# Even and odd mixers with two step slots a projection tile, another order of columns and heads, score buffers by item, and keys scaled by logarithm and exponential

## The chip, the cores and the metric

The kernel runs on one core of a Trainium2 chip. The metric is the device time of one execution in microseconds. The engines are TensorE (PE, with its weight loads PEld), VectorE (DVE), ScalarE (ACT), GpSimd (POOL) and SyncE (SP), which issues the DMA transfers here. Each engine runs its own instructions strictly in the order of the program; waits between engines are on semaphores.

## What is computed

Two blocks of a transformer run one after the other on 256 tokens of 1024 channels, all in float32. The first block has a convolution layer and a dilated attention layer, each followed by a gated feed-forward (gu0/dn0, gu1/dn1). The second block, which the change touches, is

```python
h = rms_norm(x, g) * (1 + scale) + shift        # scale, shift from "ada", a product of the condition
x = x + gate * (mixer(h) @ w_out)               # layer 0: even mixer, layer 1: odd mixer
x = x + gate2 * swiglu(...)                     # gu2/dn2 and gu3/dn3

def even_mixer(h):   # 23 tiles of 128 columns
    # 4 differential heads: two queries, two keys of 64, RMS-normed; a = softmax(1) - lam * softmax(2)
    # 8 sparse heads: one shared key and value; keys are picked by an index score (8 heads of
    #   relu(iq . ik) * iw, top 64 of each row)
def odd_mixer(h):    # 12 tiles; 16 heads, 4 shared keys and values, window of 128, one sink each
```

In both mixers every query and key vector of 64 is divided by its root mean square before the scores.

## The kernel before

Every product is `product(name, ...)`. The weights stand in one long list of 128x128 blocks; 8 blocks make a unit. SyncE loads a unit into `raw`, ScalarE rounds it into `whi` (`highs`, line 793), VectorE forms the remainder `wlo` (`lows`, line 1144). TensorE forms each block of a product from three matmuls (line 486): high by high, low by high, high by low. A tile is 128 output columns; with 8 blocks in its contraction it takes 24 matmuls. The first `lead` tiles of a product (2 in the mixers and their output products) are computed block row by block row together, since the parts of their input arrive one after another; the later ones follow one by one. The mixers use three PSUM banks for tiles, two for scores, one for norms and transposed values, one for transposes, one for weighing.

The mixers, `even()` and `odd()` in each engine's program, hang attention steps onto the tiles. `AFTER_E` and `AFTER_O` are tables written by hand: for each tile number, the steps that every engine issues behind that tile. Numbers from 23 (even) and 12 (odd) on stand for the block rows of the lead tiles of the output product, `oute` or `outo`. The steps of a differential head are dscore, dexp, dfact, dturn, dweigh, dnorm, dout; of a pair of sparse heads sscore, sexp, sfact, two sturn, sweigh; index, top and pick make the selection; of a pair of odd heads score, exp, fact, two turn, weigh. Scores, transposes and weighing are TensorE's, the exponentials and the copies out of PSUM are ScalarE's, maxima, factors and remainders are VectorE's; sfact and the odd fact are multiplied by GpSimd (`factors`, line 1678).

`project(...)` handles a tile m itself. VectorE takes it out of PSUM, times the norm of its token (`taken`, line 1491), as the last thing behind tile m. ScalarE squares it in slot m+1 (`TQ`). TensorE sums the squares by a product with `bones` (line 652) behind tile m+2, or transposes a value tile (line 649). ScalarE then takes, for a query, `Ln` and `Exp` with scale -0.5, and for a key `Sqrt`; VectorE in slot m+3 multiplies the query by the result, or for a key forms the reciprocal (line 1482) and multiplies. ScalarE copies the key with its gain in slot m+4. `log_exp()` (line 853) loads the table for `Ln` and `Exp` behind slot 14 of the even mixer and slot 5 of the odd.

`total(i)` sums the squares for the token norms of the whole layer behind tile 0; ScalarE takes the root and VectorE the reciprocal (`inverse`, line 1196) before tile 0 can be taken. `shift(i)` writes two columns for the shift beside the input of a product, which the first matmul waits for. `residual` adds an output tile to X, scales it for the next product and splits it, with one weight unit's `lows` a tile. Scores lie in two buffers `eS` (even) and three `oS` (odd), transposed weights in five `eP` and six `oP`.

## Time and profile before

| | |
|---|---|
| median of 3 runs | 1331.71 us (1327.31 to 1332.41) |
| profiled execution: time, span | 1326.97 us, 1325.7 us |
| mean granted TensorE clock | 0.963 of full |
| busy: PE, DVE, ACT, POOL | 1215.2, 970.9, 657.6, 110.3 us |
| even mixer, first matmul to the first of gu2 | about 631 to 804 us |
| odd mixer, first matmul to the first of gu3 | about 1011 to 1133 us |
| DMA | 259.36 MB, mean 196 GB/s |

The span is from the first to the last instruction of the profiled execution. A clock of 1.0 is the full one, 2.4 GHz; the other level is 0.5. Busy shares over the whole span mix stages with different limits, so the rows further below are taken by stage.

### The profile page before, as it was taken

The numbers are of one execution on the slowest core, as the hardware profiler recorded it, in microseconds if no ns is written. First come the engines' busy times: TensorE is split into PE (matmuls) and PEld (weight loads), VectorE is DVE, ScalarE is ACT, GpSimd is POOL, SyncE is SP. The second block draws the span as 40 slices with busy tenths as digits, with TensorE's granted clock in tenths as the row PEclk, the third lists the DMA queues.
The fourth block names the chain that finished last, engine by engine and source line by source line (L and its number), as shares of the span: only waits on it lengthen the run. The fifth ranks groups of instructions, "written<-read, shape, count | busy, mean of one in ns | idle before, by whom it ended". The sixth has DMA issues, their size and how long they took to land.

```text
span 1325.7 us, 24775 instructions
## 1 busy us (share of the span) xinstructions
PE 1215.2 (92%) x9796; PEld 1152.7 (87%) x9796; DVE 970.9 (73%) x1860; ACT 657.6 (50%) x1139; POOL 110.3 (8%) x106
## 2 busy tenths in 40 slices
PE   4978899999998999999878788999989868999999
PEld 4957899999987999999868578999989747999999
DVE  5966598779777888879799557888876734666743
ACT  5326554444446544454566554544444845554531
POOL 2001100002001100004000121000011113100000
PEclk9999899999999999999999789999999967999999
DMA  7587687778853778778634125887855512555552
GB/s 260 158 202 101 227 303 254 258 249 277 268 172 119 229 252 265 241 254 272 201 112 139 64 68 189 260 264 241 307 181 179 161 43 66 175 186 180 188 192 65
DMA packets 81126, 259.36 MB, mean 196 GB/s; under 512 B 8904, under 2 KB 20424, under 8 KB 81012
## 3 DMA queue, kind: packets, MB, share of 16 engines
q1 hardware_dynamic: 81012, 257.79, 61.5%
q8 instruction: 78, 1.28, 0.4%
q14 instruction: 36, 0.29, 0.1%
HBM read 252.68 MB, written 5.08 MB: 194 GB/s over the span
## 4 chain that ended last, share of the span: by engine, by line
PE 70%; DVE 18%; issue 4%; ACT 3%; POOL 1%; DMA 1%; DVEq 0%; ACTq 0%
PE ps L486 62%; DVE wlo L1144 5%; DVE aacc L1150 2%; PE ps L580 1%; DVE CV L1150 1%; POOL oS L1678 1%; PE ps L584 1%; PE ps L545 1%; ACT HH L793 1%; DVE X L1150 1%; DMA raw<-wall 1%; PE ps L576 1%; PE ps L575 1%; DVE HL L1144 1%; DVE tn L1147 1%
## 5 line engine op out<-in xcount | busy, mean ns | idle before, releaser
L486 PE MATMUL ps<-HH,whi 128*128 128x256 f32 (+1 forms) x2152 | 622.8, 289 | 41.0 <-DVE HL L1144 18.4
L486 PE MATMUL ps<-HH,wlo 128*128 128x256 f32 (+1 forms) x2152 | 614.3, 285 | 0.0
L486 PE MATMUL ps<-HL,whi 128*128 128x256 f32 (+1 forms) x2152 | 613.7, 285 | 0.0
L793 ACT ACTIVATE whi<-raw 128x1024 fp32r<-128x1024 f32 x363 | 381.1, 1057 | 344.4 <-PE ps L486 339.1
L1144 DVE TENSOR_TENSOR wlo<-raw,whi 128x1024 fp32r<-128x1024 f32 x363 | 443.9, 1227 | 42.9 <-ACT whi L793 42.4
L486 PEld LDWEIGHTS ps<-HH,whi 128*128 128x128 f32 x2152 | 414.9, 193 | 56.9 <-ACT HH L793 24.5
L486 PEld LDWEIGHTS ps<-HL,whi 128*128 128x128 f32 x2152 | 414.7, 193 | 0.3
L486 PEld LDWEIGHTS ps<-HH,wlo 128*128 128x128 f32 x2152 | 414.3, 192 | 0.0
L486 PE MATMUL ps<-GH,whi 128*128 128x256 f32 x704 | 198.2, 282 | 0.6 <-DVE bcol L1370 0.5
L486 PE MATMUL ps<-GL,whi 128*128 128x256 f32 x704 | 197.4, 280 | 0.0
L486 PE MATMUL ps<-GH,wlo 128*128 128x256 f32 x704 | 197.4, 280 | 0.0
L486 PEld LDWEIGHTS ps<-GH,whi 128*128 128x128 f32 x704 | 132.8, 189 | 2.9 <-issue 1.7
L1150 DVE SCALAR_TENSOR_TENSOR aacc<-araw,cond,aacc 128x512 f32<-128x512 f32 x168 | 132.4, 788 | 3.4
L486 PEld LDWEIGHTS ps<-GL,whi 128*128 128x128 f32 x704 | 132.9, 189 | 0.0
L486 PEld LDWEIGHTS ps<-GH,wlo 128*128 128x128 f32 x704 | 132.7, 189 | 0.0
L1678 POOL TENSOR_TENSOR HL<-tn,HH 128x256 fp32r<-128x256 f32 x24 | 24.5, 1019 | 749.5 <-ACT HH L793 749.5
L1369 DVE TENSOR_TENSOR tmp<-ps,RST 128x256 f32<-128x256 f32 x88 | 37.1, 423 | 49.0 <-PE ps L486 48.4
L793 ACT ACTIVATE HH<-tn 128x256 fp32r<-128x256 f32 x68 | 28.4, 417 | 88.9 <-DVE tn L1147 84.1
L1144 DVE TENSOR_TENSOR tmp<-ps,RST 128x256 f32<-128x256 f32 x104 | 43.3, 419 | 33.8 <-PE ps L486 33.4
L1678 POOL TENSOR_TENSOR SQA<-SQA,ts 128x256 f32<-128x256 f32 x48 | 55.1, 1147 | 48.5 <-ACT ts L793 47.5
L793 ACT ACTIVATE GH<-tmp 128x256 fp32r<-128x256 f32 x88 | 35.4, 402 | 22.6 <-DVE tmp L1144 17.9
L1144 DVE TENSOR_TENSOR HL<-ps,HH 64x256 fp32r<-64x256 f32 (+1 forms) x24 | 9.5, 421 | 46.5 <-ACT HH L793 46.5
(208 smaller groups left out, 1038.2 us busy)
## 6 DMA issues: line engine op xcount, KB each, us to landing
raw<-wall SPq DMA_DIRECT2D x363, 512.0 KB, 4.3
araw<-ada SPq DMA_DIRECT2D x96, 512.0 KB, 4.7
UR<-uscr SPq DMA_DIRECT2D x24, 142.0 KB, 3.2
scratch<-bvec SPq DMA_DIRECT2D x1, 3072.0 KB
oBB<-kbias SPq DMA_DIRECT2D x16, 192.0 KB, 2.6
aTB<-scratch SPq DMA_DIRECT2D x12, 128.0 KB, 2.5
X<-x_in SPq DMA_DIRECT2D x2, 512.0 KB, 6.5
out<-X SPq DMA_DIRECT2D x8, 128.0 KB, 3.1
```

The lines of the kernel that those rows point to most:

```text
L486: ins = pe.e.matmul(o, l, r, start=(kt == p.order[0] and i == 0), stop=(kt == p.order[-1] and i == 2))
L545: ins = pe.e.matmul(bk[32 * r:32 * r + 32, 0:T], DG[j][:, 8 * r + m, :], UR[n % 3][:, r, 4 * m:4 * m + T], start=(m == 0), stop=(m == 7))
L575: pe.e.matmul(bk[:, 0:128], q[:, 0:128], k[:, 0:128], start=True, stop=True)
L576: return pe.e.matmul(bk[:, 128:384], q[:, 128:256], k[:, 0:256], start=True, stop=True)
L580: ins = pe.e.transpose(bk[:, i * P:(i + 1) * P], s[:, i * P:(i + 1) * P], ident[:, :])
L584: pe.e.matmul(o, v(0), pt[:, 0:256], start=True, stop=False)
L793: ac.then_inc(ac.e.activation(o, i, func, **kw), sem)
L1144: dv.then_inc(dv.e.tensor_tensor(o, a, b, op), sem)
L1147: dv.then_inc(dv.e.tensor_scalar(o, a, s, s2, op) if op2 is None else dv.e.tensor_scalar(o, a, s, s2, op, op2), sem)
L1150: dv.then_inc(dv.e.scalar_tensor_tensor(out=o, in0=a, scalar=s, in1=b, op0=op, op1=op2), sem)
L1369: dv.e.tensor_tensor(t[:, :], ps[:, 0:T], rooted(name)[:, :], ALU.mult)
L1678: po.then_inc(po.e.tensor_tensor(o, a, b, op), sem)
```

## The change

1. Slots: the mixers now count two slots a tile. Slot 2m lies in the middle of tile m (behind its fourth block), slot 2m+1 behind it. Slots from 46 (even) and 24 (odd) on are the block rows of the output product. The tables are built by `differ`, `sparse` and `attend` from a start slot for each head. Slot 2 is issued between the two lead tiles' end and slot 3.
2. `project`: TensorE's norm product or transpose of tile m moves to slot 2m+2, in the middle of tile m+1; ScalarE's square to slot 2m+1, `Ln`/`Exp` to 2m+2, the key copy to 2m+4; VectorE's product to slot 2m+3. `taken` stands before `project` and the steps in slot 2m+1.
3. Orders: the columns of both mixers are in another order (keys, queries and values nearer to the heads that need them), and differential and sparse heads alternate.
4. Keys use `Ln` and `Exp` as queries do; the `Sqrt` and VectorE's `reciprocal` go. `log_exp()` moves to slot 1, and the constants with lambda's exponential to slot 3.
5. Buffers: three `eS` and `eST` by item (numbered in order of scores), eight `oP`; `eIQ` and `eRL` share their memory with later buffers.
6. `oute` and `outo` have three lead tiles. `shift(i)` is issued at the start of the residual before it, and waits for less of the ada product.

```diff
-EVEN = (17, 18, 19, 20, 21, 22, 4, 5, 6, 7, 16, 0, 8, 1, 9, 2, 10, 3, 11, 12, 13, 14, 15)
-ODD = (8, 9, 10, 11, 0, 1, 2, 3, 4, 5, 6, 7)
+EVEN = (17, 18, 19, 20, 21, 22, 4, 0, 8, 5, 1, 16, 12, 9, 13, 6, 2, 14, 7, 3, 15, 10, 11)
+ODD = (8, 0, 1, 10, 2, 3, 9, 4, 5, 6, 7, 11)
...
-    Product("mixe", 23, KD, 2, banks=(0, 1, 2)), Product("oute", 8, KD, 2, banks=(0, 1, 2)),
+    Product("mixe", 23, KD, 2, banks=(0, 1, 2)), Product("oute", 8, KD, 3, banks=(0, 1, 2)),
...
-    Product("mixo", 12, KD, 2, banks=(0, 1, 2)), Product("outo", 8, KD, 2, banks=(0, 1, 2)),
+    Product("mixo", 12, KD, 2, banks=(0, 1, 2)), Product("outo", 8, KD, 3, banks=(0, 1, 2)),
...
+def differ(k, at, weigh):
+    return (chain(weigh, ("dout", k, 2), ("dnorm", k, 1), ("dweigh", k, 0))
+            + chain(at, ("dturn", k, 3), ("dfact", k, 2), ("dexp", k, 1), ("dscore", k, 0)))
+
+
+def sparse(k, at, turn=4, weigh=6):
+    return chain(at, ("sweigh", k, weigh), ("sturn", 2 * k, turn), ("sturn", 2 * k + 1, turn + 1), ("sfact", k, 2),
+                 ("sexp", k, 1), ("sscore", k, 0))
+
+
+def attend(k, at, turns=(4, 5), weigh=6):
+    return chain(at, ("weigh", k, weigh), ("turn", 2 * k, turns[0]), ("turn", 2 * k + 1, turns[1]), ("fact", k, 2),
+                 ("exp", k, 1), ("score", k, 0))
+
+
+AFTER_E = by_slot(
+    [(3, "const", 0), (13, "gain", 0)] + [(13 + k, "index", k) for k in range(4)] + [(17 + k, "top", k) for k in range(8)]
+    + [(25, "pick", 0)] + differ(0, 18, 22) + differ(1, 24, 29) + sparse(0, 28) + sparse(1, 32) + differ(2, 36, 45)
+    + sparse(2, 38, 4, 6) + differ(3, 42, 48) + sparse(3, 44))
+AFTER_O = by_slot(
+    [(3, "const", 0)] + attend(0, 6) + attend(1, 8) + attend(2, 12) + attend(3, 14) + attend(4, 18, (4, 5), 7)
+    + attend(5, 20, (3, 4), 5) + attend(6, 22, (3, 3), 4) + attend(7, 24, (3, 3), 4))
...
+            eS = [sb(f"eS{i}", [P, 2, 384], F32, st) for i in range(3)]
...
+            oP = [sb(f"oP{i}", [P, 384], F32, st) for i in range(8)]
...
+                    if kt == p.order[3] and middle and (nt == 0 or nt >= p.lead):
+                        middle(nt)
...
-                m = s - 2
-                if not 0 <= m < len(tiles.kind) or tiles.kind[m] == "plain":
+                m = (s - 2) // 2
+                if s % 2 or not 0 <= m < len(tiles.kind) or tiles.kind[m] == "plain":
...
+            def slotted(slot):
+
+                def after(nt):
+                    if nt == 1:
+                        slot(2)
+                    slot(2 * nt + 1)
+                return dict(middle=lambda nt: slot(2 * nt), after=after)
...
-            def project(tiles, s, gain, outs):
+            def project(tiles, name, s, gain, outs):
 
                 k = tiles.kind
-                m = s - 4
-                if 0 <= m < len(k) and k[m] == "key":
-                    ac.wait_ge(S.kr, 2 * tiles.no[m] + 2)
-                    pieces = outs(m)
-                    for n, (rs, o) in enumerate(pieces):
+                m = (s - 4) // 2
+                if s % 2 == 0 and 0 <= m < len(k) and k[m] == "key":
+                    ac.wait_ge(S.kr, tiles.no[m] + 1)
+                    for rs, o in outs(m):
                         ins = ac.e.activation(o, TM[m % 6][rs, :], ACT.Copy, scale=gain(m)[rs, :])
                     ac.then_inc(ins, S.kc)
-                m = s - 2
-                if 0 <= m < len(k) and k[m] != "plain":
+                m = (s - 2) // 2
+                if s % 2 == 0 and 0 <= m < len(k) and k[m] != "plain":
                     ac.wait_ge(S.bon, tiles.bank[m] + 1)
-                    q = TQ[tiles.norm[m] % 3]
                     if k[m] == "value":
                         act(outs(m), bank[5][:, 0:T].rearrange("p (a b) -> p a b", a=2), ACT.Copy, S.b5)
-                    elif k[m] == "key":
-                        act(q[:, :], bank[5][:, 0:T], ACT.Sqrt, S.b5, bias=epsb[:, 0:1], scale=1.0 / 64)
                     else:
+                        q = TQ[tiles.norm[m] % 3]
                         act(q[:, :], bank[5][:, 0:T], ACT.Ln, S.b5, bias=epsb[:, 0:1], scale=1.0 / 64)
                         ac.settle()
                         act(q[:, :], q[:, :], ACT.Exp, S.qex, scale=-0.5)
-                m = s - 1
-                if 0 <= m < len(k):
+                m = s // 2
+                if s % 2 and 0 <= m < len(k):
                     t, b = TM[m % 6], bcol[m % 6]
-                    ac.wait_ge(S.ev, slot_of("mixe" if tiles is TE else "mixo", m) + 1)
+                    ac.wait_ge(S.ev, slot_of(name, m) + 1)
                     if k[m] == "plain":
...
-                    project(TE, s, gain_of, outs)
-                    if s == TE.col[16] + 4:
                         log_exp()
+                    project(TE, "mixe", s, gain_of, outs)
...
+                if i is not None and i >= 4:
+                    shift(i)
...
-            def project(tiles, name, s, out_of):
-
-                m, k = s - 3, tiles.kind
-                if 0 <= m < len(k) and k[m] in ("query", "key"):
+            def project(tiles, s, out_of):
+
+                m, k = (s - 3) // 2, tiles.kind
+                if s % 2 and 0 <= m < len(k) and k[m] in ("query", "key"):
                     t, b, q = TM[m % 6], bcol[m % 6], TQ[tiles.norm[m] % 3]
+                    dv.wait_ge(S.qex, tiles.norm[m] + 1)
                     if k[m] == "query":
-                        dv.wait_ge(S.qex, tiles.no[m] + 1)
                         stt(out_of(m), t[:, :], b[:, 0:1], q[:, :], ALU.add, ALU.mult, S.qf)
                     else:
-                        dv.wait_ge(S.b5, tiles.bank[m] + 1)
-                        dv.then_inc(dv.e.reciprocal(q[:, :], q[:, :]), S.kr)
-                        dv.settle()
                         stt(t[:, :], t[:, :], b[:, 0:1], q[:, :], ALU.add, ALU.mult, S.kr)
...
                 def slot(s):
-                    if s < 23:
-                        lows(low_to("mixe", s))
-                    if s == 0:
+                    if s % 2 and s < 46:
+                        lows(low_to("mixe", s // 2))
+                    if s == 1:
                         dv.wait_ge(S.twa, 1)
                         dv.wait_ge(S.tot2, 1)
                         tt(TMP[8][:, :], TMP[8][:, :], bank[6][:, 0:T], ALU.add, S.twb)
                         inverse(5)
                         inverse(6)
-                    elif s <= 4:
-                        for kt in (2 * s - 2, 2 * s - 1):
+                    if s % 2 and s < 46:
+                        taken(TE, "mixe", s // 2)
+                    if s in (5, 7, 9, 11):
+                        for kt in (s - 5, s - 4):
                             dv.wait_ge(S.rst, 7)
                             dv.wait_ge(S.sq2, kt + 1)
                             stt(X[:, kt, :], X[:, kt, :], V("fin", kt), RST[0][:, :], ALU.mult, ALU.mult, S.xf)
-                    project(TE, "mixe", s, lambda m: eQK[:, EVEN[m] if EVEN[m] < 8 else EVEN[m] - 4, :])
+                    project(TE, s, lambda m: eQK[:, EVEN[m] if EVEN[m] < 8 else EVEN[m] - 4, :])
                     for w, k in AFTER_E.get(s, ()):
                         step(w, k)
-                    if s < 23:
-                        taken(TE, "mixe", s)
-
-                for s in range(23):
+
+                for s in range(46):
                     slot(s)
-                residual("oute", 5, lambda nt: mod(0, 2, nt), ALU.mult, lambda kt: slot(23 + kt))
+                residual("oute", 5, lambda nt: mod(0, 2, nt), ALU.mult, lambda kt: slot(46 + kt))
 
             def odd():
                 def step(what, hp):
                     s2, ST = oS[hp % 3], oST[hp % 3]
```

## Rows read from the trace of the kernel before

**Rows 1.** Even mixer: stretch, us; PE, PEld, DVE, ACT, POOL busy; clock, DMA, GB/s

```profile
668.00:696.40 28.40, 20.33 (x155) 17.75 (x154) 27.70 (x55) 18.46 (x32) 0.00 (x0) 0.92 0.35 112
696.40:735.00 38.60, 34.34 (x247) 30.81 (x248) 36.55 (x128) 24.48 (x64) 0.00 (x0) 0.93 0.44 135
735.00:781.60 46.60, 33.02 (x166) 23.63 (x164) 18.65 (x47) 24.05 (x72) 7.45 (x8) 0.71 0.13 44
781.60:803.60 22.00, 17.96 (x150) 17.76 (x150) 18.62 (x30) 12.62 (x25) 10.81 (x9) 1.00 0.49 150
```

**Rows 2.** The same for the odd mixer

```profile
1038.00:1060.00 22.00, 18.50 (x143) 15.43 (x142) 16.17 (x64) 16.70 (x49) 4.98 (x4) 1.00 0.54 168
1060.00:1111.40 51.40, 35.83 (x179) 24.14 (x179) 15.65 (x71) 22.60 (x73) 12.16 (x13) 0.67 0.12 39
1111.40:1132.50 21.10, 19.05 (x156) 18.71 (x156) 16.92 (x29) 13.59 (x26) 10.84 (x9) 1.00 0.44 131
```

**Rows 3.** Chain of waits (start, us, what), and TensorE's timeline

```profile
630.69 0.49 issue
...
703.57 2.87 PE ps L486 x24
...
706.66 0.43 PE ps L575 x4
707.09 0.43 PE ps L576 x4
...
711.12 1.14 DVE wlo L1144
...
1021.01 0.45 PE L652 MATMUL ps<-tmp,bones 128*128 128x256 f32 x1 [0.36 <-ACT tmp L793]
```

**Rows 4.** ScalarE's timeline: start us, us, instruction

```profile
638.12 1.28 ACT L793 ACT_TABLE_LOAD   x1
...
1043.26 0.49 ACT L793 ACTIVATE tmp<-tmp,bcol 128x256 f32<-128x256 f32 x1
1043.65 0.39 ACT L793 ACTIVATE oS<-oS,oST 128x128 f32<-128x128 f32 x1
...
1045.51 1.05 ACT L793 ACTIVATE whi<-raw 128x1024 fp32r<-128x1024 f32 x1
```

**Rows 5.** VectorE's timeline in both mixers

```profile
668.00 1.75 DVE L1482 RECIPROCAL tmp<-tmp 128x256 f32<-128x256 f32 x1
...
693.45 0.62 DVE L1519 MAX8 eM<-eSW 128x8 f32<-128x128 f32 x2
...
694.77 0.41 DVE L1491 TENSOR_TENSOR tmp<-ps,RST 128x256 f32<-128x256 f32 x1
...
707.73 0.17 DVE L1554 RECIPROCAL eST<-eST 128x4 f32<-128x4 f32 x1
...
709.33 0.28 DVE L1390 CUSTOM_DVE_ANT_0 eS<-ps,eBB 128x128 f32<-128x128 f32 x1
...
740.71 1.01 DVE L1150 SCALAR_TENSOR_TENSOR eS<-eDS,ps 128x384 f32<-128x384 f32 x2
...
742.88 0.42 DVE L1491 TENSOR_TENSOR tmp<-ps,RST 128x256 f32<-128x256 f32 x1
...
1066.52 0.41 DVE L1491 TENSOR_TENSOR tmp<-ps,RST 128x256 f32<-128x256 f32 x1
```

**Rows 6.** GpSimd's and VectorE's timeline while both work

```profile
1050.55 2.60 POOL L1678 TENSOR_TENSOR oS<-oS,oST 128x256 f32<-128x256 f32 x2 [46.25 <-DVE oST L1637]
...
1050.78 1.47 DVE L1144 TENSOR_TENSOR wlo<-raw,whi 128x1024 fp32r<-128x1024 f32 x1
1052.17 1.26 DVE L1150 SCALAR_TENSOR_TENSOR oQ<-tmp,bcol 128x256 f32<-128x256 f32 x1
```

**Rows 7.** VectorE's first residual instruction in each mixer's tail

```profile
782.24 0.48 DVE L1150 SCALAR_TENSOR_TENSOR X<-ps,MOD,X 128x256 f32<-128x256 f32 x1 [0.71 <-PE ps L486]
...
1113.01 0.48 DVE L1150 SCALAR_TENSOR_TENSOR X<-ps,MOD,X 128x256 f32<-128x256 f32 x1 [0.72 <-PE ps L486]
```

More of the change, by code:

```diff
@@ L199, with chain @@
[L199 to L207 removed]
+def chain(at, *steps):
+    return [(at + later, what, k) for what, k, later in steps]
@@ new lines, in by_slot @@
+def by_slot(steps):
+    slots = {}
+    for s, what, k in sorted(steps, key=lambda x: x[0]):
+        slots.setdefault(s, []).append((what, k))
+    return slots
+def differ(k, at, weigh):
[4 more added lines that the diff above has]
+                 ("sexp", k, 1), ("sscore", k, 0))
@@ L258, with counted, item @@
 STEPS_O = [x for s in sorted(AFTER_O) for x in AFTER_O[s]]
-SCORES_E = [(w, k, g) for w, k in STEPS_E if w in ("index", "dscore", "sscore") for g in range(2)]
-BANK6_E = [x for x in STEPS_E if x[0] in ("dturn", "dnorm", "sturn")]
-BANK7_E = [(w, k) for w, k in STEPS_E if w in ("dweigh", "sweigh")]
+def counted(**by):
+    n, at = 0, {}
+    for what, k in STEPS_E:
+        if what in by:
+            n += by[what]
+            at[what, k] = n
+    return at
+SCORES_E = [(w, k, g) for w, k in STEPS_E if w in ("index", "dscore", "sscore") for g in range(2)]
+ITEMS_E = counted(dscore=1, sscore=1)
+EM_E = counted(dscore=5, sscore=5)
+EX_E = counted(dexp=4, sexp=4)
+FACT_E = counted(dfact=6, sfact=1)
+TURNED_E = counted(dturn=1, sturn=1)
+BANK6_E = counted(dturn=1, dnorm=1, sturn=1)
+WEIGHED_E = counted(dweigh=1, sweigh=1)
+YHH_E = counted(dout=1, sweigh=1)
+BANK7_E = counted(dout=1, sweigh=1)
+def item(what, k):
+    return ITEMS_E[what[0] + "score", k // 2 if what == "sturn" else k] - 1
 class Queue:
@@ L707, in step @@
+                    if what == "sweigh":
+                        for g in range(2):
+                            pe.wait_ge(S.b6, BANK6_E["sturn", 2 * k + g])
+                            ins = weigh(bank[7][rows64(g), 0:T], lambda tt: eV[:, tt, 512:576],
+                                        eP[(TURNED_E["sturn", 2 * k + g] - 1) % 5])
+                        pe.then_inc(ins, S.ewe)
                     if what == "dnorm":
-                        pe.wait_ge(*free6(AT_BANK6[what, k]))
+                        pe.wait_ge(S.b6, BANK6_E[what, k] - 1)
@@ L718, in after, with slot @@
-                def after(s):
-                    if s == 0:
+                def slot(s):
+                    if s == 1:
                         total(4)
@@ L772, in after @@
                         step(w, k)
-                product("mixo", HH[NORM_SET[6]], HL[NORM_SET[6]], T + 2, norm_ready(6), after)
-                product("outo", HH[YO_SET], HL[YO_SET], T, lambda kt: pe.wait_ge(S.ohl, kt + 1), None, lambda kt: after(12 + kt))
+                product("mixo", HH[NORM_SET[6]], HL[NORM_SET[6]], T + 2, norm_ready(6), **slotted(slot))
+                product("outo", HH[YO_SET], HL[YO_SET], T, lambda kt: pe.wait_ge(S.ohl, kt + 1), None, lambda kt: slot(24 + kt))
             convolution()
@@ L1114, in slot @@
                 def slot(s):
-                    if s < 12:
-                        highs(split_to("mixo", s))
-                    if s == 0:
+                    if s % 2 and s < 24:
+                        highs(split_to("mixo", s // 2))
+                    if s == 1:
                         norm_root(6)
-                    project(TO, s, gain_of, outs)
-                    if s == TO.col[9] + 4:
                         log_exp()
+                    project(TO, "mixo", s, gain_of, outs)
                     for w, k in AFTER_O.get(s, ()):
                         step(w, k)
-                for s in range(12):
+                for s in range(24):
                     slot(s)
-                residual("outo", 7, lambda kt: slot(12 + kt))
+                residual("outo", 7, lambda kt: slot(24 + kt))
             convolution()
@@ L1617, in step @@
                     M, NM, DEN, FA, SE = (ST[:, i, :] for i in range(5))
+                    if what == "const":
+                        gains(1, 1)
+                        tt(gqk[:, 2:3], V("qnc"), V("knc"), ALU.mult, S.gqk)
+                        dv.wait_ge(S.mm, end_mm("dn2"))
+                        for i in range(2):
+                            dv.then_inc(dv.e.tensor_copy(oSK[:, :, i:i + 1], row[:, 256:272].unsqueeze(2)), S.sk)
                     if what == "score":
```

239 lines of the change are left out of this document (100 added, 139 removed).

## The prediction

> **What bounds it now.** I read the table of stretches first. The even mixer [rows 1] and the odd one [rows 2] are where TensorE is less than full; the feed-forward stages between them are solid matmul. In the even mixer three regimes follow each other. From 668 to 735 us VectorE is busy 64 of 67 us: it sets the pace. From 735 to 781.6 us no engine is full (TensorE 33 of 46.6, VectorE 18.7), the granted clock averages 0.71, and what ends last is a chain of attention steps. From 781.6 to 803.6 VectorE works through the residual. The odd mixer shows the same: 51.4 us at a clock of 0.67, with the projections mostly done and the heads following one behind the other.
>
> Then the chain of waits and the engines' timelines, for prices [rows 3 to 5]. TensorE: a tile is 8 blocks, 24 matmuls, 2.87 us; a pair of score products 0.86. VectorE, counted from start to start so that overlap isn't paid twice: a weight rest (wlo) 1.13, taking a tile 0.41, one round of the top-k 1.32, the differential factors 1.6, the sparse scores 2.17, a key's reciprocal 1.75. ScalarE: the exponentials of one head pair 1.86.
>
> **The change, part by part.**
>
> *Keys by logarithm and exponential.* The reciprocal of 1.75 us leaves VectorE for 5 keys in the even and 2 in the odd mixer: 12.2 us of VectorE work, against one more ScalarE instruction of about 0.4 us per key. The even ones fall in the stretch where VectorE sets the pace, so this is a real gain, about 8.7 us, inside the sum below. In the odd mixer VectorE is not full [rows 2], and it is worth little.
>
> *Tables and shifts.* The load of 1.28 us at 638.12 [rows 4] goes, since lambda's exponential moves behind the square roots. ScalarE would still wait for VectorE's sum there, so I count 0.35 us to 0.8 us. The shift columns are now written ahead of the residual: the 0.49 us of issue at 630.69 [rows 3] is two tiny VectorE instructions in front of the first matmul, and the same stands in front of gu2, mixo and gu3. Four times 0.49. The start of the even mixer thus comes 0.85 us earlier by the time tile 3 starts (the two gains overlap in part).
>
> *Two slots a tile.* This is the heart, and it has a price. Before, the norm matmul of tile m stood after tile m+2, so TensorE had two tiles of work while VectorE took the tile and ScalarE squared it. Now it stands in the middle of tile m+1: 1.44 us after the end of tile m. VectorE takes tile m behind the steps of slots 2m-1 and 2m and a weight rest; if those include factors that wait for an exponential, a loop closes: square of tile m-1 (0.45), exponentials (1.86), factors (0.2 sparse or 1.6 differential), scores if any (1.33 or 2.17), weight rest and taking (1.54), back to the square of tile m. That is 4.2 to 9 us with hops of 0.05, against 3.3 to 6 us of TensorE work in the same tile.
>
> I followed the even order through. VectorE takes tile 6 at about 658.5 (one step of the ada product lies ahead of it). Tiles 7 to 12, where top-k rounds and differential head 0 fill VectorE: 5.6, 5.9, 6.8, 5.8, 6.1, 7.0 us, sum 37.2. Six tiles with the loop (13, 15, 17, 19, 20, 22): 5.5, 4.7, 6.6, 9.5, 4.7, 9.0, sum 40.0. Four where VectorE waits for scores placed in a tile's middle (14, 16, 18, 21): 5.4, 7.8, 5.3, 6.9, sum 25.4; two of these hold an ada step of 1.45. One of them spelled out, tile 19: square 0.45, copy of a transpose 0.4, exponentials 1.86, logarithm and exponential of a query norm 0.83, copy of a weighed head 0.3 on ScalarE, then on VectorE its rest 0.34, factors 1.6, sparse scores 2.17, weight rest and taking 1.54: 9.5. (ScalarE's single instructions on 256 columns count 0.3 to 0.45, by the one of 0.49 in [rows 4], overlap taken off.) All together 102.6, so tile 22 is taken at 761.1 instead of 742.88 [rows 5]: 18.2 us later.
>
> But only one differential head and two half-done sparse ones are then left. From 761.1: ScalarE's identity, square, copy, exponentials and two norm instructions, then head 2's product, split and rest, 5.2 us, to 766.3; head 3's weighing, square, norm and split behind it, 4.1, to 770.4; block row 3 (1.1), the last sparse head (1.3) and block rows 4 to 7 (4.3), to 777.1. The last factors on GpSimd (2.6 us [rows 6]) run beside it. 16.0 us to the end of the lead of 24 blocks. Before it was 39.4 us, from 742.88 to the first residual at 782.24 [rows 7]. So the lead ends 5.2 us earlier.
>
> *Three lead tiles.* The residual is paced by VectorE: 21.4 us from 782.24 to the end of the last stretch of [rows 1], for 8 tiles, 6 weight rests and an ada step. With three lead tiles one rest (1.13) is done before the lead ends, and the shift's 0.3 to 0.5 is gone: -1.4 us. All three banks are then full, so TensorE waits about 0.5 us for the first residual; VectorE's list is longer anyway (20 us against 14.2 for five tiles), which hides it. Even mixer: -6.6 us.
>
> *Odd mixer.* Here is a new wait. The first tile is a key, and its norm matmul stands in slot 2, straight behind the two lead tiles. Before, tile 2 was computed while the root, the reciprocal and the square of tile 0 ran, and even then the matmul came 0.36 us after TensorE was free, at 1021.01 [rows 3]. Now TensorE waits some 3.0 us with tile 2 still ahead of it. The even mixer starts with plain tiles and is spared. Then the loop again, head by head: the tiles are taken at about 1031.9 (tile 3), 1038.2, 1042.8, 1050.1, 1058.2, 1062.7, 1072.2, 1080.3 and 1086.3, against 1066.52 for the last before [rows 5]: 19.8 us later. From there, half of the heads being done, 22.1 us to the end of the lead at 1108.4, against 46.5 us (1066.52 to 1113.01, [rows 5, 7]): 4.6 us earlier. The residual gives 1.6 as above. Odd mixer: -6.2 us.
>
> *At no cost:* the score buffers by item (three instead of two) remove waits that in my walk are never last; oP with 8 buffers likewise; moving the bias loads on the sync queue keeps them ahead of weight loads that are several tiles early (DMA share 0.35 to 0.44, [rows 1]). If a bias load were late, its head would wait for the landing once.
>
> *GpSimd beside VectorE.* Factors now run beside weight rests and residual products. A product of 0.48 us took 1.26 beside them [rows 6]: +0.78 us at most, 12 times, 0 to 9 us; I take 0.3 each where it lies in a loop, within the walk. The Trainium skill ("SBUF — State Buffer", SBUF: two separate sides) says the port pair shared by VectorE and GpSimd is an exclusive lock, the loser waiting out the whole instruction. The row agrees for the second product, which ends just behind GpSimd; by the rule alone every such meeting could cost up to a full GpSimd instruction.
>
> *Clock.* At 0.5 of the full clock a tile costs twice 2.87. The stretch from 668 to 735, with TensorE about three quarters occupied, kept 0.92 to 0.93 [rows 1]; the new tiles are as dense (about 77 us of TensorE work in 102). I add 1.5 us.
>
> **Sum.** 1326.97 (the profiled execution's own time) - 6.6 - 6.2 + 1.5 = 1315.7. That execution is at the low end of the runs shown (median 1331.71), which by itself asks for up to 4 us more; I say 1316.
>
> **Rivals.**
>
> *The loops hide.* If ScalarE and VectorE run ahead more than my walk lets them, each tile costs only the larger of its TensorE and VectorE lists: about 85 instead of 102.6 us in the even mixer, some 12 us less in the odd one. Then 1316 - 29 = 1287, or half of it, 1300. For it: both lists sum to about 122 us by the prices above, for a mixer of 173 us (630.69 to 803.60, [rows 1, 3]). Against it: every queue is strictly in order, and each factor step stands ahead of a taking.
>
> *No change.* The tiles lengthen by 18 to 20 us in each mixer and the tails shorten by 23 to 24; these are differences of large terms. Two more microseconds on each of six loop tiles, or the full 9 us beside GpSimd, and nothing is left: 1325 to 1335. The port rule ends here too (0.03 of the 0.15 below): if each of the 12 pairs of GpSimd products, 2.6 us by [rows 6], held VectorE up for 1.5 us, that is 18 us, and 1334. This is the mechanism that the page just named describes.
>
> *Slower: the clock.* The gaps of 2 to 3 us in every tile pull the granted clock down, as between 1060 and 1111 us [rows 2]. If the new stretches (102 and 59 us, with 77 and 45 us of TensorE work) ran at 0.75, the work would take 26 and 15 us more; about 40% of it would fall into gaps, so +24: 1340. It decides from a mean clock of about 0.87 there.
>
> **Chances.** Forecast, 1305 to 1325: 0.45. Loops hidden, below 1305: 0.30. No change: 0.15. Slower: 0.10. Half a per cent, 6.7 us, is about what a measurement of this kernel tells from nothing: faster 0.75, same 0.15, slower 0.10. The range 1291 to 1333 leaves about 0.1 on each side.
>
> **What would show it.** Right: no reciprocal on keys; one idle gap of about 3 us on TensorE near 1017, ended by the first square; gaps of 1 to 3 us in the middle of most mixer tiles, released by ScalarE's square; tile 22 taken near 761; a tail of about 16 us in place of 39; residuals 20 and 18 us. Wrong: no gaps in the tiles (1300 or less); a clock under 0.87 from 690 to 770; a load of tables inside the mixers; or a tail still above 25 us.

## The result, and the profile after

The changed kernel takes 1319.81 us (median of 5 runs, 1318.96 to 1324.01), the kernel before 1331.71 (its five runs lie between 1327.31 and 1332.41); the ratio is 0.9929, interval 0.9911 to 0.9947, which is 9.5 us. The profiled execution took 1320.58 us, with a span of 1319.2 and a mean granted clock of 0.972. The forecast was 1316 in a range of 1291 to 1333, so time, sign and range held. Of the steps behind it the walk through the tiles held, and the price of the joints and the length of the tails did not.

First the table of stretches (columns as in [rows 1]), three of the even mixer and one of the odd. A joint below is the place where one product ends and the next begins.

```profile
668.00:700.00 32.00, 21.74 (x149) 19.03 (x147) 29.57 (x106) 16.78 (x42) 0.00 (x0) 0.95 0.36 111
700.00:735.00 35.00, 30.34 (x209) 25.54 (x209) 19.93 (x49) 20.50 (x55) 5.22 (x4) 0.90 0.34 103
735.00:782.00 47.00, 34.65 (x229) 29.79 (x230) 24.58 (x62) 24.91 (x64) 5.22 (x4) 0.89 0.28 84
...
1082.00:1109.30 27.30, 21.29 (x128) 16.87 (x129) 7.77 (x26) 12.93 (x35) 4.11 (x4) 0.75 0.22 67
```

VectorE was busy 64 of 67 us from 668 to 735 us in the kernel before [rows 1]. Now it is busy 29.6 of the first 32 us and 19.9 of the 35 behind them: no engine is full from 700 us on. But the even mixer's lead (the first tiles of its output product, which run together) does not end earlier. VectorE's timeline, last tile taken and first residual in each mixer (compare [rows 5, 7]):

```profile
762.65 0.42 DVE L1532 TENSOR_TENSOR tmp<-ps,RST 128x256 f32<-128x256 f32 x1
...
782.12 0.48 DVE L1194 SCALAR_TENSOR_TENSOR X<-ps,MOD,X 128x256 f32<-128x256 f32 x1 [1.76 <-PE ps L521]
...
1081.34 0.42 DVE L1532 TENSOR_TENSOR tmp<-ps,RST 128x256 f32<-128x256 f32 x1
...
1109.26 0.48 DVE L1194 SCALAR_TENSOR_TENSOR X<-ps,MOD,X 128x256 f32<-128x256 f32 x1 [2.18 <-PE ps L521]
```

Tile 22 is taken 20 us later than before, and the tail shrank from 39.4 to 19.5 us: the first residual moved by 0.1 us. What TensorE waited for from 640 to 782 us, the two largest entries (us in total, times, longest):

```profile
PE ps L689 <- ACT tmp L840: 14.3, 10, 2.8
PE ps L686 <- ACT tmp L840: 7.3, 4, 3.7
```

L689 is the norm matmul in the middle of the next tile, L686 the transposition of a value tile in the same place; both wait for ScalarE's square or identity, and ScalarE's own wait for VectorE's taking is 43.1 us in 16 gaps in the same stretch. In the odd mixer L689 waits 11.7 us in six gaps, the first of them where the prediction put it:

```profile
1015.97 0.70 PE L689 MATMUL ps<-tmp,bones 128*128 128x256 f32 x2 [3.14 <-ACT tmp L840]
```

The two profiled executions differ by 6.5 us of span. Cut at the same instructions, the difference lies as follows. R is the start of the reciprocal of a stage's norm (where one row stands for two of them, its start), X an instruction that adds a product to the residual.

| from, to | before | after | difference |
|---|---|---|---|
| start to dn1's last X (nothing changed) | 628.96 | 630.40 | +1.44 |
| dn1's last X to mixe's R | 11.00 | 8.62 | -2.38 |
| mixe's R to oute's first X | 142.28 | 143.10 | +0.82 |
| oute's eight X | 19.59 | 18.50 | -1.09 |
| oute's last X to gu2's R | 13.36 | 11.28 | -2.08 |
| gu2 and dn2 (nothing changed) | 193.42 | 193.89 | +0.47 |
| dn2's last X to mixo's R | 9.36 | 7.24 | -2.12 |
| mixo's R to outo's first X | 95.04 | 96.23 | +1.19 |
| outo's eight X | 17.65 | 17.05 | -0.60 |
| outo's last X to gu3's R | 11.83 | 9.75 | -2.08 |

So in the profile the mixers proper got 2.0 us *longer*, the residuals 1.7 us shorter, and the four joints 8.7 us shorter, which is more than the whole difference. The prediction had priced the shift at 0.49 us each. The stages that nothing changed differ by up to 1.4 us, so single differences of that size are not to be read. The chain of waits in front of gu2 shows the new joint:

```profile
800.70 0.41 DVE X L1194
...
801.15 9.35 PE ps L521 x63
```

The first matmul follows the last X directly. Before, gu2's first matmul stood at 804.11, 2.28 us after the start of the last X at 801.83: behind X came its gain, ScalarE's split, VectorE's rest, and only then the shift, which stood last in VectorE's queue. TensorE needs the shift columns for its first matmul, the last X's rest only for its last block. The position is the cause and not the looser wait for the ada product: in the kernel before, the shift at 803.52 follows the rest at 803.18 without a gap.

### The profile page after: what moved, and what is told of

Its sections match the earlier page's. It is cut to its first block, busy times and chain, and to the rows that moved or that the text cites. A ratio compares the mean times of both kernels' runs of the same rounds, so it can differ in the third digit from the quotient of the medians.

```text
span 1319.2 us, 24769 instructions
## 1 busy us (share of the span) xinstructions
PE 1213.2 (92%) x9796; PEld 1152.0 (87%) x9796; DVE 959.4 (73%) x1853; ACT 653.0 (49%) x1142; POOL 109.0 (8%) x106
## 3 DMA queue, kind: packets, MB, share of 16 engines
q8 instruction: 78, 1.28, 0.4%
## 4 chain that ended last, share of the span: by engine, by line
PE 70%; DVE 18%; ACT 5%; issue 3%; DMA 1%; POOL 0%; DVEq 0%; ACTq 0%
PE ps L521 63%; DVE wlo L1188 6%; DVE CV L1194 1%; PE ps L582 1%; DVE X L1194 1%; DVE aacc L1194 1%; ACT HH L840 1%; DMA raw<-wall 1%; PE ps L617 1%; ACT tmp L840 1%; ACT oS L840 1%; DVE tmp L1532 1%; PE ps L621 1%; DVE HL L1188 1%; PE ps L689 1%
## 5 line engine op out<-in xcount | busy, mean ns | idle before, releaser
L840 ACT ACTIVATE tmp<-tmp,bcol 128x256 f32<-128x256 f32 x74 | 37.1, 501 | 64.5 <-DVE bcol L1533 63.4
```

The source lines that it names most:

```text
L840: ac.then_inc(ac.e.activation(o, i, func, **kw), sem)
```

## Experiments

The ratios are to the kernel before, run beside each kernel on the same chip.

**1. The two edits at the joints alone**, in the kernel before:

```diff
-    Product("oute", 8, KD, 2, banks=(0, 1, 2)),
+    Product("oute", 8, KD, 3, banks=(0, 1, 2)),
...
-    Product("outo", 8, KD, 2, banks=(0, 1, 2)),
+    Product("outo", 8, KD, 3, banks=(0, 1, 2)),
...
-    dv.wait_ge(S.amod, 3 if i < 6 else 6)
+    dv.wait_ge(S.amod, {4: 1, 5: 2, 6: 4, 7: 5}[i])
...
 def residual(name, i, scale, op, before=None):
     p = PROD[name]
+    if i is not None and i >= 4:
+        shift(i)
...
-                if f >= 2:
-                    shift(i)
...
-                shift(4)
...
-                shift(6)
```

> The kernel before with only the two edits at its stages' ends: three lead tiles for both output products, and the four shifts written ahead of the residual. No slots, no new order, keys as before. By the prediction's ledger this is worth 4 x 0.49 us for the shifts and about 1 us for each third lead tile: 4 us, a ratio to the kernel before of 0.997. By the comparison of the two profiled executions it is worth nearly all of the change: from the first residual to gu2's first matmul 21.9 us became 19.0, in front of gu3 19.9 became 17.6, in front of mixo 1.3 to 1.6 us went, 0.3 in front of mixe: 6.5 to 7 us, a ratio of 0.995 or below.

Measured: 0.9879 (0.9857 to 0.9902), 1314.5 us. That is 16 us, four times the prediction's ledger, and more than the whole change.

**2. The shifts alone** (two lead tiles as before).

> The kernel before with the four shifts ahead of the residual alone, two lead tiles as before. With the third lead tile too it was 0.988, 16 us shorter. By the chain in front of gu2 and gu3 the shift is worth 1.8 us at each of four places, 7 us, and up to 4 us more where the pause of 2.3 us in front of the first matmul halved the clock for the next 3.4 us: 0.992 to 0.995. Then the third lead tile brought the other 6 us, by keeping TensorE's clock up in the tails (granted 0.85 and 0.83 instead of 0.71 and 0.67). If all of it is the shift, 0.988.

Measured: 0.9889 (0.9869 to 0.9909). So it is nearly all the shift, 14.8 us; the third lead tile adds 0.001, within the uncertainty. In the profile each of the four joints is 2.1 us shorter, 8.3 us; the two mixers behind them are 2.5 and 2.8 us shorter as well, without any edit in them. The traces show where. VectorE takes the tiles at the same distances from R, to within 0.2 us, except at two places. In the even mixer TensorE pauses 2.28 us in front of the fourth tile in both kernels, until the first is out of its bank. Behind this pause the kernel before runs at half clock and this one at full clock (table of stretches, before and then this kernel):

```profile
644.07:647.07 3.00, 3.00 (x14) 3.00 (x15) 3.00 (x8) 2.69 (x4) 0.00 (x0) 0.50 0.00 0
```

```profile
641.96:644.96 3.00, 3.00 (x25) 3.00 (x26) 3.00 (x8) 2.70 (x4) 0.00 (x0) 1.00 0.00 0
```

By the sixth tile that is 1.3 us. In the odd mixer it is a pause for GpSimd's factors, 1.86 us before 1060.26 and 1.84 us before 1051.17, with a clock of 0.52 and 1.00 in the 3 us behind it: 1.5 us. The remaining 1.3 us of each mixer lie in the tails, where the last part ran at 0.80 and 0.89 in the even mixer and at 0.65 and 0.77 in the odd one. So the 5.3 us go with the granted clock; why it stayed up is open (last section).

**3. The shifts back**, in the changed kernel.

```diff
-    dv.wait_ge(S.amod, {4: 1, 5: 2, 6: 4, 7: 5}[i])
+    dv.wait_ge(S.amod, 3 if i < 6 else 6)
...
-    if i is not None and i >= 4:
-        shift(i)
...
+                if f >= 2:
+                    shift(i)
...
+                shift(4)
...
+                shift(6)
```

> The changed kernel with the four shifts back at the start of mixe, gu2, mixo and gu3. By the prediction's ledger 4 x 0.49 = 2 us longer than the changed kernel (ratio to the kernel before 0.9945 instead of 0.993). The rival: the shift stands last in VectorE's queue, so with it the first matmul waits for the residual's last gain, split and rest as well, 1.8 us at each place by the chain in front of gu2 (802.32 to 804.11): 5 to 7 us longer, ratio 0.997 to 0.998.

Measured: 1.0036 (1.0021 to 1.0050), 1332.5 us: slower than the kernel before, and 14 to 16 us above the changed one. The rival held for gu2 (1.86 us longer) and was too small for the others: mixe 3.57, mixo 3.55, gu3 4.19. The further part stands where the clock fell behind the pause. TensorE's timeline at mixe, and the table of stretches (columns as in [rows 1]) there:

```profile
631.86 0.55 PE L521 MATMUL ps<-HH,whi 128*128 128x258 f32 x1 [2.27 <-DVE HL L1188]
```

```profile
632.00:635.00 3.00, 3.00 (x14) 3.00 (x15) 2.96 (x4) 0.55 (x1) 0.00 (x0) 0.50 0.85 319
635.00:638.00 3.00, 3.00 (x26) 3.00 (x26) 0.37 (x1) 1.06 (x1) 0.00 (x0) 0.97 0.80 277
```

After the pause TensorE runs at half clock, 1.2 instead of 2.4 GHz, for about 3 us: 14 matmuls in 3 us, and 26 in the next three. The changed kernel, whose pause there is 0.16 us, keeps 1.00. At mixo the first 3 us run at 0.50 as well, and at gu3 at 0.50 and the next 3 at 0.77. These are the clocks of one execution; the ratio, over all runs of this kernel, has the same size.

**4. Two lead tiles** in the changed kernel.

> The changed kernel with two lead tiles in the two output products instead of three. By the prediction 1 us each, 2 us longer (0.9945). If the shift is what shortened the tails, 0.5 to 1 us each, 1.0 to 1.5 us longer (0.994). If the third tile's 8 blocks gave TensorE work that kept the head chain company without lengthening it, no difference.

Measured: 0.9891 (0.9871 to 0.9912), against 0.9929 and, beside the kernels of experiments 2, 6 and 7, 0.9913 (0.9891 to 0.9934; the changed kernel run again, below). Not longer; perhaps shorter. In its profile the lead ends 140.2 and 92.5 us behind R instead of 143.1 and 96.2, and the eight X take 1.1 and 0.6 us more. The residual one weight rest shorter is there, but in the changed kernel eight more blocks, 2.87 us of matmuls [rows 3], stand ahead of the first X. Without slots (experiments 1 and 2) the lead with the third tile ended 0.6 and 2.6 us earlier, not later, at a clock of 0.85 instead of 0.72 from 735 us to the even mixer's first residual; by the ratios neither can be told from nothing.

**5. The keys as well**: experiment 1 with the keys' roots by logarithm and exponential, still with the old order and one slot a tile.

```diff
-    elif k[m] == "key":
-        act(q[:, :], bank[5][:, 0:T], ACT.Sqrt, S.b5, bias=epsb[:, 0:1], scale=1.0 / 64)
...
-        dv.wait_ge(S.b5, tiles.bank[m] + 1)
-        dv.then_inc(dv.e.reciprocal(q[:, :], q[:, :]), S.kr)
-        dv.settle()
...
+    log_exp()    # behind the roots of slot 0 in each mixer
```

> The same with the keys' roots by logarithm and exponential on ScalarE as well, in the old order and with one slot a tile. By the prediction the five reciprocals of 1.75 us leave a stretch in which VectorE sets the pace, 8.7 us of gain, so the ratio to the kernel before falls from 0.997 to about 0.990. The rival: the chain of the last attention heads ends last and begins with scores whose place is bound to TensorE's tiles, so VectorE's time comes back as idle time: within 2 us of the kernel with the ends alone, 0.995.

Measured: 0.9806 (0.9782 to 0.9829), 1302.3 us: the fastest kernel of the study, 9.7 us (0.0073) below experiment 1 and 14 to 16 us below the changed kernel. In the profiles the lead ends 129.0 us behind R in the even mixer, against 139.2 in experiment 1, and 89.5 against 89.7 in the odd one. The table of stretches:

```profile
668.00:700.00 32.00, 29.32 (x222) 26.77 (x222) 30.39 (x95) 19.99 (x43) 0.00 (x0) 0.95 0.47 156
700.00:735.00 35.00, 26.60 (x191) 22.75 (x191) 28.80 (x95) 23.92 (x67) 0.00 (x0) 0.97 0.35 112
```

Here VectorE is still busy 59 of 67 us, and TensorE 29.3 of the first 32, against 21.7 of the changed kernel in the same stretch.

The 10.2 us are not the reciprocals alone. With the keys' `Sqrt` ScalarE has to load tables in the middle of the even mixer, which the prediction had not priced. In the trace of experiment 1 there are loads at 688.93, 690.72 and 696.77, ScalarE's timeline and then what TensorE does behind them:

```profile
690.72 1.28 ACT L793 ACT_TABLE_LOAD   x1
...
692.97 0.66 PE L649 MATMUL ps<-ident,tmp 128*128 128x128 f32 x2 [3.67 <-ACT tmp L793]
```

The value tile's identity stands behind two of these loads, 2.6 us, and TensorE waits 3.67 us for it. In experiment 5 the loads and this wait are gone. A further 1.2 us of the 10.2 is the clock behind the pause of 2.28 us, 0.50 in experiment 1 and 1.00 here. The shares were not separated in this kernel; experiment 6 prices the reciprocals without the loads, in the other one.

**6. The keys' reciprocals back**, in the changed kernel.

```diff
-    act(q[:, :], q[:, :], ACT.Exp, S.qex, scale=-0.5)
+    act(q[:, :], q[:, :], ACT.Exp, S.qex, scale=0.5 if k[m] == "key" else -0.5)
...
+    dv.then_inc(dv.e.reciprocal(q[:, :], q[:, :]), S.kr)
+    dv.settle()
     stt(t[:, :], t[:, :], b[:, 0:1], q[:, :], ALU.add, ALU.mult, S.kr)
```

> The changed kernel with the keys' reciprocals of 1.75 us back on VectorE (the exponential on ScalarE then gives the root instead of its inverse, so ScalarE's work stays). In the kernel with one slot a tile their removal was worth 9.6 to 14 us. If they are worth as much here as there, 9 us and more longer than the changed kernel, 1.000. If in the slotted kernel VectorE is no longer what sets the pace (29.6 and 19.9 us busy of 32 and 35 between 668 and 735 us, against 30.4 and 28.8), only those in a loop count, about 3 of 7: 5 us, 0.997.

> The changed kernel itself, unedited, as the yardstick for the kernels beside it on this chip. Its ratio was 0.993; every theory expects 0.991 to 0.995.

Measured: 0.9995 (0.9980 to 1.0009) against the changed kernel's 0.9913 on the same chip: 10.9 us, uncertain by 3 to 4, for seven reciprocals of 1.75 us, 12.3 us in all; the spans of the two profiled executions differ by 6.2, of which 3.9 lie in the even mixer, 1.4 in the odd one and 1.5 at gu3's joint. So half of them or more count, though VectorE is far from full. That they count because they lie in the loop that closes a tile is the likely reading, and it is not shown by itself.

**7. The norm matmul one slot later**, with ScalarE's and VectorE's part of it.

```diff
 # TensorE
-    m = (s - 2) // 2
-    if s % 2 or not 0 <= m < len(tiles.kind) or tiles.kind[m] == "plain":
+    m = (s - 3) // 2
+    if s % 2 == 0 or not 0 <= m < len(tiles.kind) or tiles.kind[m] == "plain":
...
 # VectorE
-    m, k = (s - 3) // 2, tiles.kind
-    if s % 2 and 0 <= m < len(k) and k[m] in ("query", "key"):
+    m, k = (s - 4) // 2, tiles.kind
+    if s % 2 == 0 and 0 <= m < len(k) and k[m] in ("query", "key"):
```

> The changed kernel with each norm matmul and value transposition one slot later, behind tile m+1 instead of in its middle, and what ScalarE and VectorE do with it one slot later; all steps of the heads stay where they are. If the loop of square, exponentials, factors, scores and taking is closed by the early norm matmul, its waits on ScalarE's square (14.3 us in ten gaps in the even mixer, 11.7 in six in the odd one) shrink by 1.44 us each: 15 to 20 us shorter than the changed kernel, ratio 0.980. If each tile is held up by what stands in front of its taking on VectorE anyway, only the odd mixer's first wait of 3.1 us shrinks: 1 to 3 us shorter, 0.991.

Measured: 1.0042 (1.0025 to 1.0060), 17 us longer than the changed kernel beside it; both expectations missed. The waits for the square go, and others take their place in the even mixer (640 to 795 us, the two largest):

```profile
PE ps L621 <- ACT eV L840: 7.7, 2, 5.1
PE ps L612 <- DVE eQK L1194: 6.0, 5, 2.9
```

The scores and weighings stand where they stood, and the queries and values they need now come one slot later. The table of steps leaves no slack between a projection and its first use. The experiment therefore doesn't price the early norm matmul by itself.

**8. The old table of steps, spread over the slots**, in the changed kernel, with the old and with the new order of columns. Both also get one more load of odd biases, `load_bo(7)`, which the old table needs.

```diff
-AFTER_E = by_slot(...)
-AFTER_O = by_slot(...)
+AFTER_E = {2 * s + 1 if s < 23 else 23 + s: x for s, x in OLD_E.items()}
+AFTER_E[3] = [("const", 0)]
+AFTER_O = {2 * s + 1 if s < 12 else 12 + s: x for s, x in OLD_O.items()}
+AFTER_O[3] = [("const", 0)]
```

> The changed kernel with its two slots a tile, early norm matmul, score buffers, shifts, third lead tile and keys, but with the old order of columns and heads and the old table of steps, every old slot standing in the odd slot behind its tile (15 to 30 us of TensorE and VectorE work between the steps of one head instead of half tiles). If the denser table is what costs (a head's scores, exponentials and factors of some 6 us within half tiles of 1.44 us of matmuls), this comes near the kernel with ends and keys alone: 0.981, with the last tile taken 90 to 95 us after the norm's reciprocal and not 124. If the early norm matmul costs (a wait for ScalarE's square in the middle of each tile), it stays at 0.990 to 0.992, with those waits still 10 us and more.

> The same, with the new order of columns and of the odd heads' tiles. If the order alone does little, as the one above within 2 us (0.981 or 0.991 by the same two theories). If the new order costs (keys and queries of the heads come later than the old table wants them), 5 us and more longer than the one above.

Measured: 0.9903 (0.9876 to 0.9929) with the old order, 0.9886 (0.9861 to 0.9911) with the new one. Neither theory is met in full. The last tile of the even mixer is taken 97.1 and 95.5 us behind R, as the first theory wanted, and the lead ends 136.7 and 135.0 us behind it, not 129 as in experiment 5 and not 143.1. So by the profile the dense table costs some 6 to 8 us of the even mixer. By the ratios the second kernel is 4 to 6 us below the changed kernel, uncertain by 4, and 11 us above experiment 5; the two orders don't differ measurably. In the odd mixer the lead ends 92.7 us behind R with the new order and 96.6 with the old one, against 89.5 in experiment 5 and 96.2 in the changed kernel. With the new order TensorE's waits there, from 1007 to 1100 us, are those of experiment 5 but for one:

```profile
PE ps L637 <- POOL oS L1739: 17.8, 8, 3.6
PE ps L709 <- ACT tmp L860: 3.1, 1, 3.1
```

In experiment 5 the first wait is 17.7 us in eight gaps and the norm matmul waits 0.4 us. The new wait of 3.1 us is as large as the 3.2 us between the two kernels.

**9. Taking the tile behind the steps of its slot**, as the kernel before did, in the second kernel of experiment 8 and in the changed kernel. I had come to think that taking first was the cost.

```diff
 # VectorE, even mixer; the odd one alike
-    if s % 2 and s < 46:
-        taken(TE, "mixe", s // 2)
...
     for w, k in AFTER_E.get(s, ()):
         step(w, k)
+    if s % 2 and s < 46:
+        taken(TE, "mixe", s // 2)
...
 # ScalarE: square, or identity, of the tile
-    m = s // 2
-    if s % 2 and 0 <= m < len(k):
+    m = (s - 2) // 2
+    if s % 2 == 0 and 0 <= m < len(k):
```

> The kernel with two slots, the old table of steps and the new order (0.989), with VectorE taking tile m behind the steps of its slot, as the kernel before did, and ScalarE's square or identity of it one slot later. If taking first is what costs (a head's factors on VectorE stand behind a tile that TensorE hasn't finished, and its exponentials on ScalarE behind the square of that tile), this comes to the kernel with ends and keys alone, 0.981 to 0.984, 7 to 10 us shorter, with the odd mixer's lead 90 us behind the reciprocal instead of 92.7 and the even one's 128 instead of 135. If the early norm matmul costs, it gets worse, since the square now comes later still and TensorE waits for it in each tile: 0.992 or above.

> The same edit in the changed kernel itself (0.991 to 0.993), with its dense table of steps. By the theory that taking first costs: 5 to 10 us shorter, 0.985 to 0.988. By the prediction's loop (square, exponentials, factors, scores, weight rest, taking, square again, closed by the norm matmul in the middle of the next tile): the square then stands behind one or two more steps, each tile's wait grows by 1 to 2 us, 15 us longer or more, 1.003.

Measured: 1.0056 (1.0036 to 1.0077) with the old table of steps, 0.9992 (0.9978 to 1.0007) in the changed kernel: 23 and 8 to 11 us longer. That theory fell, and the prediction's loop gained, though in the changed kernel it had asked for 15 us or more. With one step more between a tile and its square, the norm matmul of the first kernel waits, from 640 to 800 us,

```profile
PE ps L709 <- ACT tmp L860: 18.4, 11, 2.9
PE ps L706 <- ACT tmp L860: 9.0, 5, 3.9
```

27.4 us, where without the edit L709 waited 2.5 us in three gaps. In the changed kernel the two kinds of wait rise from 21.6 to 28.4 us.

## Why the number was right, and which of its reasons were

**Shifts and joints** (four times 0.49 us, the table load within them): the mechanism was seen and its size missed by four to seven and a half times. The prediction costed the two tiny instructions and not the queue that they stood at the end of. Measured: 2.1 us at each joint by the profile, 14.8 us in all by the ratio of experiment 2, 14 to 16 us by experiment 3. Of that, 8.3 us are the joints themselves in experiment 2 and 5.3 us a higher clock in the mixers; in experiment 3 some 6 of 13.2 us are half clock (estimate: the four joints less 1.86 us each). By the table above the joints gave 6.7 us more than the 1.96 us of the four shifts, and 6.3 more with the prediction's 0.85 us for shift and table load together at mixe.

**Keys** (8.7 us in the even mixer, little in the odd): right in size, 9.7 us (0.0073, uncertain by 0.003) in experiment 5, and by the profile 10.2 in the even mixer and 0.2 in the odd one. The mechanism is right in part: VectorE's takings do come faster, but the 10.2 us also hold three table loads that the prediction had not counted, and 1.2 us of clock. That the sum agrees so well is partly luck.

**The table load** of 1.28 us at 638.12 [rows 4] is gone from that place: lambda's exponential stands behind the roots. One load is still there, at 639.37, beneath the reciprocal of 3.37 us, where nothing waits for it. By the table above the whole joint gave 2.38 us against 2.08 to 2.12 at the three that have no table load: 0.3 us for it, just below the 0.35 to 0.8 expected.

**Two slots a tile, even mixer.** Tile 22 was forecast at 761.1 and taken at 762.65, so the walk through the loop held, and not by luck: tiles 13 to 22 took 5.5, 5.9, 4.3, 8.3, 6.8, 6.1, 9.5, 4.4, 7.5 and 8.9 us, where 5.5, 5.4, 4.7, 7.8, 6.6, 5.3, 9.5, 4.7, 6.9 and 9.0 had been forecast. (The upper end of the loop, given as 9 us, adds up to 7.6 by the terms named.) The step that failed is the tail, "16.0 us to the end of the lead": it took 19.5. It was 6.5 us to the end of head 2's rest (5.2 forecast), 5.5 to the end of head 3's (4.1) and 7.5 to the end of the lead (6.7). The clock there was 0.82, so the 15.3 us of busy TensorE are longer by some 2.8 us than at full clock, an estimate, where the sum had 1.5 us for both mixers. One block row of nine matmuls took 2.18 us behind a pause of 2.29, and another 1.07 at full clock. With the start of the mixer 0.9 us earlier, the first residual came 5.0 us later than forecast. And the walk was compared with the wrong kernel: against the kernel before it included the keys' 9 us. Against experiment 5, which has everything but the slots, the new table, the order and the buffers, the even mixer is 14 us longer in the profile (143.1 against 129 us behind R).

**Odd mixer.** The wait in front of tile 0's norm matmul was forecast at 3.0 and is 3.14 us. The last tile is taken 68.3 us behind R, where 1086.3 - 1017.5 = 68.8 had been forecast. From the last taking, 22.1 us to the lead's end were forecast; it took 27.9. The gain of 4.6 us, 0.5 of it the earlier start, became a loss of 1.2 behind R, and against experiment 5 it is 6.8. In this tail the last two heads go one step at a time: for the last one exponentials 1.75 us, factors 2.5 on GpSimd, two transpositions with a copy each. The clock was 0.75, which makes the 21.3 us of busy TensorE longer by an estimated 5.3 us.

**Together** the slots and what belongs to them cost 0.011 to 0.012 of the time, 14 to 16 us (0.9806 against 0.9913 and 0.9929), where the ledger had them as a gain. Experiment 8 gives 4 to 6 us of this, uncertain by 4, to the dense table of steps; the new wait in the odd mixer is 3 us. The rest, some 6 us, lies mostly in the even mixer between experiments 5 and 8: 1.3 us up to the last taking and 4.7 us in the tail (39.5 against 34.8, at clocks of 0.87 and 0.85, so the clock is not the reason). It is not assigned to an edit. Experiment 9 shows that the loop through the early norm matmul is sharp, not how much it costs where it is; a kernel with the norm matmul and all steps moved together was not tried.

**Third lead tile** (-1.4 and -1.6 with the shift): the residuals are 1.1 and 0.6 us shorter, the first as the 1.13 us of one weight rest had it and the second half of that. By experiments 2 and 4 nothing measurable is left of it.

**GpSimd beside VectorE** (0.3 us each, and the rival by which VectorE is held up 1.5 us at each pair): VectorE lost next to nothing, GpSimd did. Their timelines in the changed kernel:

```profile
1056.48 1.20 DVE L1188 TENSOR_TENSOR wlo<-raw,whi 128x1024 fp32r<-128x1024 f32 x1
...
1056.65 2.50 POOL L1719 TENSOR_TENSOR oS<-oS,oST 128x256 f32<-128x256 f32 x2 [4.70 <-DVE oST L1684]
...
1050.34 1.61 POOL L1719 TENSOR_TENSOR oS<-oS,oST 128x256 f32<-128x256 f32 x2 [10.58 <-DVE oST L1684]
```

The weight rest kept its time; the pair beside it took 2.50 us, and 1.61 where VectorE was reading scores from the banks. What differs from the kernel before is who started first. Here the weight rest had begun 0.17 us ahead of the pair, and GpSimd paid 0.9 us; there the pair had begun 0.23 us ahead of the weight rest [rows 6], and VectorE paid, with 1.47 instead of 1.22 us and then 1.26 instead of 0.48. The Trainium skill ("SBUF — State Buffer", SBUF: two separate sides) says that whichever of the two starts first gets the port pair for the whole instruction and the other fully blocks. Both cases agree; a cost of 18 us to VectorE is not there. GpSimd's 0.9 us is not free either: the last pair of the odd mixer, at 1096.71, took 2.50 us behind a weight rest and lies on the chain that ends the lead.

**Clock** (+1.5): 0.89 to 0.90 from 700 to 782 us, but unevenly, 0.94 from 735 to the last taking and 0.82 in the tail. The slower rival, through a mean clock below 0.87, did not come in the even mixer; in the odd one's last 27 us it was 0.75, where the kernel before had 0.67 over its last 51 us [rows 2].

**The rivals.** The loops didn't hide: TensorE has its gaps. "No change" was nearly true of the mixers, for the reason that it gave: differences of large terms.

So the total was met because two errors cancelled in part, which is luck: by the profile the joints gave 6 to 7 us more than written down, and the two leads ended later than forecast, the even one by 5.0 us (782.12 against 777.1), the odd one by 5.3 (96.2 us behind R, where 1108.4 - 1017.5 = 90.9 had been forecast). What did not cancel is 4.9 us, the profiled 1320.58 against the sum of 1315.7.

## What to carry to other kernels

When a small instruction is moved away from the front of a stage, price the whole queue behind which it stood, up to the first instruction that waits for it, and the clock behind the pause; here two instructions of 0.2 us at each of four joints were worth more than the rewriting of both mixers. Compare each part of a change with the kernel that has all the others: a tail that shrinks from 39 to 20 us is no gain if the last tile comes 20 us later. And a step whose result goes back to the engine that feeds it (tile, taking, square, norm matmul) needs as much of that engine's work in between as the way round takes: with 1.44 us of matmuls in between TensorE waited 21.6 us in the even mixer, though what the early place costs in all was not isolated. When a function is replaced, look in the trace for the table loads that go with it. Of the parts tried, moved shifts, the third lead tile and keys by logarithm and exponential with the old slots are the best: 1302 us.

## What the runs showed of the hardware

The same pause of TensorE doesn't always have the same effect on its clock. In front of mixe it was 2.26 us in the kernel before and 2.27 in experiment 3. Before, the stretch from 631 to 634 us ran at 1.00, with 23 matmuls:

```profile
631.00:634.00 3.00, 2.82 (x23) 2.85 (x24) 2.16 (x10) 2.38 (x3) 0.00 (x0) 1.00 0.84 288
```

in experiment 3 the corresponding one ran at 0.50. The same holds for mixo (2.32 and 2.33 us, clocks of 1.00 and 0.50 from 1011 to 1014). Nor does the program decide it. The pause inside the even mixer shows this: in front of the fourth tile it is 1.97 us in the changed kernel, which then ran at 1.00, and 1.97 us in experiment 4, which has the same program up to there and ran at 0.54 in the 3 us behind it. So the profile of one execution can hold about 1.3 us of clock, at such a pause, that the next one doesn't have. In front of gu2 all three kernels pause longer, 4.55 us before, 2.69 in the changed kernel and 5.72 in experiment 3, and all three lose clock in the first 3 us: 0.55, 0.67 and 0.52. That fits the 1.86 us, the chain's own, that experiment 3 lost at gu2. In front of gu3 the pauses are 2.50, 1.98 and 4.20 us, and the clocks behind them 1.00, 1.00 and 0.50.

A load of ScalarE's tables took 1.28 us each time, and the next instruction began 0.02 us behind it (688.93, 1.28 us, then 690.23, in experiment 1).
